# Four re-orderings in a two-layer decoder trunk: memory heads' products inside the last RWKV chunk, two low-part subtractions on POOL, POOL's bonus work gated by VectorE's splits, and five smaller moves

## The reference

```python
for i in range(DEPTH):
    hn = rmsnorm(h, pre_mix_g[i])
    if i % 2 == 0:
        proj = hn @ nsa_w_in[j];   prim = nsa_mixer(...)
    else:
        proj = hn @ rwkv_w_in[j];  prim = rwkv7_time_mix(...)
    mo = memory_attention(proj[..., -MEM_WIDTH:], mem_k, mem_v)
    mix = jnp.concatenate([prim, mo], axis=-1) @ w_out[i]
    h = h + rmsnorm(mix, post_mix_g[i])
    gu = rmsnorm(h, pre_ffn_g[i]) @ w_ffn_in[i]
    ff = (jax.nn.silu(gu[..., :FFN_HIDDEN]) * gu[..., FFN_HIDDEN:]) @ w_ffn_out[i]
    h = h + rmsnorm(ff, post_ffn_g[i])
```

## Time and profile before

| | us |
|---|---|
| median of 3 runs | 733.96 (733.24 to 736.04) |
| the profiled execution's own time | 732.03 |
| its span | 729.9 |
| PE busy | 701.5 (96%) |
| DVE busy | 478.2 (66%) |
| ACT busy | 407.1 (56%) |
| POOL busy | 128.8 (18%) |
| PE clock granted | 0.998 of full |
| one weight piece split: ACT's high part, DVE's low part (means) | 1.88, 2.28 |
| from one 512-column matmul to the next on PE, output products | 0.23 |

### The profile page before, as it was taken

The page is one execution under the profiler, slowest core; times in us unless marked ns, Lnnn a source line. Parts: engine busy times, 40 slices in busy tenths (PEclk is TensorE's granted clock), DMA queues, the critical chain, the costliest instruction groups (busy, mean ns, idle before and its releaser), DMA issues.

```text
span 729.9 us, 14047 instructions
## 1 busy us (share of the span) xinstructions
PE 701.5 (96%) x5949; PEld 606.7 (83%) x5949; DVE 478.2 (66%) x673; ACT 407.1 (56%) x667; POOL 128.8 (18%) x175
## 2 busy tenths in 40 slices
PE   8999989999999999999999999888999999999996
PEld 7879965778888888888889989887789888888885
DVE  4697788747866756633666987985668775666323
ACT  4753868647664554532798945433268555455411
POOL 8111067700000000000180066930000000000000
PEclk9999999999999999999999999999999999999999
DMA  9946810008656555545573531000075665555511
GB/s 303 347 149 200 290 59 2 1 1 276 215 182 206 190 172 190 213 174 172 189 230 116 174 117 60 5 3 4 1 248 188 203 199 173 181 209 187 178 54 57
DMA packets 78288, 111.63 MB, mean 153 GB/s; under 512 B 2140, under 2 KB 64754, under 8 KB 78226
## 3 DMA queue, kind: packets, MB, share of 16 engines
q1 hardware_dynamic: 77170, 107.68, 44.1%
q0 software_dynamic: 976, 3.04, 1.3%
q10 hardware_dynamic: 80, 0.02, 0.0%
HBM read 109.68 MB, written 1.05 MB: 152 GB/s over the span
## 4 chain that ended last, share of the span: by engine, by line
PE 84%; DVE 7%; ACT 4%; issue 2%; POOL 1%; DMA 1%; ACTq 0%; DVEq 0%; POOLq 0%
PE ps L1074 20%; PE ps L746 14%; PE ps L747 13%; PE ps L748 13%; PE ps L1077 10%; DVE w_lo L1925 2%; ACT w_hi L1465 2%; PE ps L1249 2%; PE ps L1267 2%; PE ps L929 2%; PE ps L903 1%; PE ps L878 1%; DMA rows_a<-pre_ffn_g 1%; POOL chunk_x L728 1%; PE ps L1275 1%
## 5 line engine op out<-in xcount | busy, mean ns | idle before, releaser
L1925 DVE TENSOR_TENSOR w_lo<-w_raw,w_hi 128x2048 fp32r<-128x2048 f32 (+3 forms) x102 | 231.5, 2283 | 102.0 <-ACT w_hi L1465 101.9
L1465 ACT ACTIVATE w_hi<-w_raw 128x2048 fp32r<-128x2048 f32 (+3 forms) x102 | 189.4, 1877 | 50.0 <-PE ps L748 45.3
L1074 PE MATMUL ps<-x_hi_lo,w_hi 128*128 128x512 f32 x640 | 201.2, 396 | 0.0
L1077 PEld LDWEIGHTS ps<-x_hi_lo,w_lo 128*128 128x128 f32 x640 | 120.2, 188 | 28.4
L1077 PE MATMUL ps<-x_hi_lo,w_lo 128*128 128x256 f32 x640 | 125.7, 278 | 0.0
L1074 PEld LDWEIGHTS ps<-x_hi_lo,w_hi 128*128 128x128 f32 x640 | 97.4, 189 | 0.0
L746 PE MATMUL ps<-w_hi,x_hi_lo 128*128 128x512 f32 (+3 forms) x240 | 83.0, 346 | 6.1 <-DVE x_hi_lo L2145 4.4
L747 PE MATMUL ps<-w_lo,x_hi_lo 128*128 128x512 f32 (+3 forms) x240 | 81.0, 337 | 0.0
L748 PE MATMUL ps<-w_hi,x_hi_lo 128*128 128x512 f32 (+3 forms) x240 | 81.0, 337 | 0.0
L746 PE MATMUL ps<-w_hi,hidden_hi 128*128 128x512 f32 x176 | 68.6, 390 | 0.0
L747 PE MATMUL ps<-w_lo,hidden_hi 128*128 128x512 f32 x176 | 68.5, 389 | 0.0
(11 more groups left out here) (378 smaller groups left out, 1063.4 us busy)
## 6 DMA issues: line engine op xcount, KB each, us to landing
w_raw<-w_ffn_in SPq DMA_DIRECT2D x44, 1024.0 KB, 5.1
w_raw<-w_ffn_out SPq DMA_DIRECT2D x22, 1024.0 KB, 4.9
w_raw<-rwkv_w_in SPq DMA_DIRECT2D x11, 1024.0 KB, 5.7
w_raw<-w_out SPq DMA_DIRECT2D x8, 1024.0 KB, 4.9
w_raw<-nsa_w_in SPq DMA_DIRECT2D x6, 1024.0 KB, 13.8
w_raw<-nsa_cmp_k_w SPq DMA_DIRECT2D x2, 1024.0 KB, 5.4
w_raw<-nsa_cmp_v_w SPq DMA_DIRECT2D x2, 1024.0 KB, 5.4
w_raw<-nsa_w_in SPq DMA_DIRECT2D x2, 768.0 KB, 4.8
```

Of the source, the lines that this page charges most:

```text
L1074: pe.matmul(psum[:, bank + j, :], kt_of(w_hi, i, k)[:, cols[j]], xx[:, k, :, :].rearrange("p c n -> p (c n)"), start=k == 0, stop=False)
L1077: ins = pe.matmul(psum[:, bank + j, 0:SEQ], kt_of(w_lo, i, k)[:, cols[j]], xh[:, k, :], start=False, stop=k == KD - 1)
L1465: act.activation(w_hi[:, i % SPL, 0:size(i)], raw[:, i % RAW, 0:size(i)], ACT.Copy).then_inc(hi_done, 1)
L1925: dve.tensor_tensor(w_lo[:, i % RAW, 0:size(i)], raw[:, i % RAW, 0:size(i)], w_hi[:, i % SPL, 0:size(i)], ALU.subtract).then_inc(lo_done, 1)
```

## The change

- PE, last chunk: the memory heads' twelve matmuls for tile 0 are taken out of `out_pieces([(0, 0)])` and spread: three before the wait for `k_zs`, three behind `turn_y(1)` (itself moved ahead of the wait for `k_us`), six behind the last y product. `turn_y(2)` moves from before piece (1, 0) to behind it.
- ACT and DVE, last chunk: `high(0)` moves to right behind the copy of z, `high(1)` ahead of `gn_square(3)`; `finish_lo(0)`, `finish(1)` and `finish_lo(1)` move ahead of `gn_mean(3)`.
- Joins 0 and 2: the low part of the second strip's piece is made by POOL (`low_part`), and DVE only waits for its count later.
- All three joins: tile 1's transposes move from behind tile 0's strips to before the last six matmuls of the second of them.
- POOL's bonus work waits until DVE has made the low parts of the two pieces in front of W1.
- ACT does one split, the four A copies, and then the other two splits.

The hunks below stand in the order of the file: POOL's program, PE's, ACT's, DVE's.

```diff
+            def low_part(i):
+                pool.wait_ge(hi_done, i + 1)
+                pool.wait_ge(lo_done, i)
+                pool.tensor_tensor(w_lo[:, i % RAW, 0:size(i)], raw[:, i % RAW, 0:size(i)], w_hi[:, i % SPL, 0:size(i)],
+                                   ALU.subtract).then_inc(lo_done, 1)
...
             scale_probs(0)
+            low_part(first["out", 0] + N_OUT + 1)
             load_gain(1)
...
             pool.wait_ge(g_ev, 3)
+            pool.wait_ge(lo_done, first["rwkv"] + 11 + 3 + AHEAD - 1)
             for f in range(FT):
                 ins = pool.tensor_scalar(rT[:, f, :], rT[:, f, :], colB[:, B_LNB + f:B_LNB + f + 1], None, ALU.add)
...
             ins.then_inc(gb_ok, 1)
+            low_part(first["out", 1] + N_OUT + 1)
             load_gain(3)
...
                         pe.wait_ge(j_lo, tile_base(m, t) + k // 2 + 1)
+                    if t == 0 and part == 1 and k == KD - 2:
+                        norm_tile(m, 1)
...
                 for t in range(TT):
-                    if t:
-                        norm_tile(m, t)
                     for part in range(2):
...
+            def memory_rows(part, nh):
+                kk = 2 * OUT_PAIRS[1][0] + part
+                three(psum[:, acc_bank(2, 0) + nh, :], xh[:, kk, tile(0)], xl[:, kk, tile(0)],
+                      kt_of(w_hi, first["out", 1], part)[:, HALVES[nh]], kt_of(w_lo, first["out", 1], part)[:, HALVES[nh]],
+                      start=part == 0, stop=False)
...
-                if c >= 3:
-                    pe.wait_ge(y_fin_ok, c - 2)
+                if c == NCH - 1:
+                    pe.wait_ge(lo_done, first["out", 1] + 1)
+                    memory_rows(0, 0)
+                    pe.wait_ge(y_fin_ok, 1)
                 pe.wait_ge(k_zs, c + 1)
                 each(U_BANK, inv(c), z_in).then_inc(k_u, 1)
...
+                if c == NCH - 1:
+                    turn_y(1)
+                    memory_rows(1, 0)
                 pe.wait_ge(k_us, c + 1)
...
-                if c == 3:
-                    turn_y(1)
-            out_pieces([(0, 0)])
+            memory_rows(0, 1)
+            memory_rows(1, 1)
+            pe.wait_ge(y_lo, 2)
+            out_pieces([(1, 0)])
             turn_y(NCH - 2)
-            pe.wait_ge(y_lo, 2)
-            out_pieces([(1, 0), (2, 0)])
+            out_pieces([(2, 0)])
             turn_y(NCH - 1)
...
-            split_to(first["rwkv"] + 11 + 3)
+            split_to(first["rwkv"] + 11 + 1)
...
                 act.activation(x2[:, c, 0], six(2 * c), ACT.Copy).then_inc(pa[c], 1)
+            split_to(first["rwkv"] + 11 + 3)
...
                 act.activation(by_pair(zt[:]), crossed(z_at(c)), ACT.Copy).then_inc(k_zs, 1)
+                if c == NCH - 1:
+                    high(0)
...
-            high(0)
+            high(1)
             gn_square(NCH - 1)
-            high(1)
             gn_root(NCH - 1)
...
                     if t == 0:
-                        split_to(last_piece + 2)
                         first_half(m, 1)
                     tile_lo(m, t)
+                if m != 1:
+                    dve.wait_ge(lo_done, last_piece + 2)
+                    split[0] += 1
                 split_to(last_piece + 5)
...
                     finish(0)
+                if c == NCH - 1:
+                    finish_lo(0)
+                    finish(1)
+                    finish_lo(1)
                 gn_mean(c)
                 if c:
                     gn_scale(c - 1)
-            finish_lo(0)
-            finish(1)
-            finish_lo(1)
             gn_variance(NCH - 1)
```

## The result

| | before | after |
|---|---|---|
| median, executions of the comparison | 733.96 (732.06 to 736.04, 5) | 723.35 (722.86 to 725.32, 5) |
| ratio to before, 95% interval | | 0.9852 (0.9835 to 0.9869) |
| the profiled execution: own time, span | 732.03, 729.9 | 725.32, 723.6 |
| its granted clock | 0.998 | 0.994 |

The kernel became 10.6 us faster by the medians.

What follows compares the result with a forecast made beforehand. PE's own work was taken to bound the kernel, so only its idle time could be won. Terms -2.8, -2.4, -0.3, -2.95 and +0.1 gave -8.3: 732.03 to 723.7, plus 1.9 for the median, 725.7 us; range 723.7 to 729.8.

Steps and rivals of the forecast that it cites:

- Part 1: Last chunk: memory products fill PE's four gaps, together 2.93 us, and DVE's new order keeps up; -2.8 (-1.4 to -2.9).
- the late y: Last chunk: the last y product starts at about 511.5 instead of 510.95, 0.5 us late.
- both covers: Last chunk: inputs ready just ahead of PE, by 0.15 us at piece (1, 0) and 0.2 at tile 1.
- part 4: Ahead of W1: with POOL's bonus work later, DVE's splits shorten and PE's wait of 2.97 goes; -2.95 (0 to -3.0).
- Parts 2 and 3: Joins: POOL's low parts and earlier transposes win 1.2 each in joins 0 and 2; transposes win 0.3 in join 1.
- Part 5: Ahead of V1: POOL may issue before DVE's splits, V1's first sum then starting later; +0.1 (-0.3 to +0.5).
- (a): Last chunk gives back half, `y_lo` of 2 and 4 being late: -1.4 in place of -2.8, 727.1; chance 0.15.
- (b): Joins 0 and 2: POOL's low part ends late and delays `h` of tile 1; 729.1 us, chance 0.08.
- (c): Ahead of W1: part 4 does nothing, or bonus work holds W1 or the masks; 728.7 us, chance 0.06.
- (d): Joins 0 and 2: POOL's low part takes 10.6 us, each join loses 4.4; slower, 736.8 us, chance 0.03.
- (e): Whole kernel: low bounds of all terms, some 0.5 us more, with the medians' scatter; 724.5 us, chance 0.05.
- the clock theory: From the experiments: PE's long gaps also bring falls of the granted clock, costing 1.6 us more; no chance given.

Runs made afterwards that it cites:

- experiment 6: Kernel after with four extra POOL subtractions of 256 columns ahead of POOL's low part in joins 0 and 2: 728.5 us, those joins 2.22 longer each.
- experiment 2: Kernel after with POOL's bonus work no longer held back: 727.84 us in one run.
- experiment 1: Both kernels again, unaltered: after 722.87 us, ratio 0.9854; before 733.99 us, ratio to itself 1.0006.
- experiment 4: Kernel after with the last chunk and the start of the output product in the order of before: 728.06 us.
- experiment 8: Kernel before with idle matmuls ahead of W1's consumers alone, 734.08 us, or in the last chunk alone, 733.9; kernel after with POOL's bonus work ungated, 728.13.
- the kernel with both fills: Kernel before with 18 unread identity matmuls in PE's gaps, 12 ahead of W1's consumers and 6 in the last chunk: 732.5 us, ratio 0.9977.
- experiment 7's second kernel: Kernel after with the last chunk in the order of before, timed again: 726.09 us (725.66 to 727.44).
- both single fills: Kernel before with only the 12 idle matmuls ahead of W1's consumers, 734.08 us (ratio 1.0008), or only the last chunk's 6, 733.9 (1.0003).

## Why the prediction was right in kind and too small

- **Part 1, last chunk** (-2.8): all four gaps filled, the late y as described, both covers held. Measured -3.09. The term was mis-sized by 0.29: it took the gaps at their brackets, 2.93, less 0.15 for changes of shape. A bracket counts from the modelled end of the last matmul, and a row of 0.39 whose successor starts 0.23 later shows that this end can lie 0.16 behind the point from which the next could have started. The one gap of part 4 shows it plainly: 2.97 by its bracket, 3.12 won. How much of the 0.29 is this and how much the 0.15 isn't shown. The Trainium skill (Perfetto Trace Analysis, "Tensor Engine Instruction (MATMUL, LD_WEIGHTS)") says that this end is an estimate, and the rows agree.
- **Parts 2 and 3, joins** (-1.2, -0.3, -1.2): measured -1.16, -0.25, -1.15. POOL's instruction was sized by subtracting the wait inside a row (4.5, measured 4.61); the plain proportion of the same row would have said 6.7, an ending 2.1 later than the measured one, and experiment 6 shows what an ending 2.7 later costs.
- **Part 4** (-2.95): measured -3.12, for the same reason as part 1. The cause of the long split was named rightly: experiment 2 undoes it.
- **Part 5** (+0.1): measured -0.21. The order of the two engines was foreseen, its effect not: the price was put on DVE's first sum, but PE's path goes over POOL's fourth product, which ends 0.3 earlier. The forecast took that end for unchanged.
- **Rivals (a) to (d)** didn't occur: no wait in the last chunk, none for POOL's low part, no cover lost. Rival (e), more than forecast, is what came; its 724.5 was still 1.15 too high.
- **The step that failed** is the last of the sum: "it lay 1.9 below the median of the runs, 733.96, from which the prediction goes". These 1.9 us were carried over whole to the kernel after, as if every kernel's median lay that far above its undisturbed execution. Over all executions the kernel before has its median 2.27 above its fastest (733.98 against 731.71, 75 executions; the profiled one, at 732.03, was among its fastest tenth), the kernel after only 0.82 (722.90 against 722.08, 9 executions).
- **The 2.35 us in full**: 0.65 are the terms (-9.0 measured, -8.35 forecast), 0.45 lie outside the span, where the sum had no term at all, 0.09 are two roundings up (8.35 to 8.3, 725.6 to 725.7), and 1.16 are left for the carried distance, the start up to join 0 included.
- **Why the distance shrank** is in part argued. That some executions with these gaps pay for a fall of the clock right behind them is seen in traces (experiments 1, 2, 4 and 8), and the executions at a mean clock of 0.990 or less, 21 of 70 before, are absent from the kernel after and from the kernel with both fills. Against it stand the timings of experiment 7's second kernel and of both single fills: none came out as the clock theory had it. Falls ahead of join 0 are a second source: 7 of the 16 profiles have one at 96 to 107 us, kernels with the change among them, so with nine executions of the kernel after a part of the difference may be chance.

Left open: why one fill alone has no effect, why the same gap is followed by a fall in some executions and not in others, and what shortens the time outside the span. The low end of the range should have held the result: 723.7 was the forecast's own figure for the profiled execution, without room for the terms' small errors to add up.

## What to carry to other kernels

When one profile lies at the edge of the times of its kernel, the distance from the median isn't a constant that a change leaves alone: look at the granted clock in windows of several profiles, and at the time outside the span, before carrying either over. When DVE and POOL both work from SBUF, read an overlong row as work plus a wait for the other engine's instruction, subtract the wait before pricing the row elsewhere, and find which engine's last instruction the path goes over; here the pair ahead of W1, pulled apart, gave 3.1 of its 3.2 us of waiting, and one split less ahead of V1 gave 1.3 of 2.0. A cover of 0.3 us was enough, but beyond it the loss was nearly one for one.

## What the hardware did that I had not expected

- The granted clock of a PE that is 96% busy falls to 0.50 (1.2 of 2.4 GHz) for some 3 to 7 us, in part of the executions of the same program. In two profiles it came about 1 us behind gaps of 1.06 to 1.08 and 0.54 (experiments 1, 4), in two at the end of one of 2.96 (experiments 2, 8), at a price of 1.5 to 1.6 us each. Others lay at 8 to 15 us (3 of the 16 profiles) and at 96 to 107 us (7 of them), in stretches whose code the change doesn't touch; those profiles reach join 0 up to 3 us later than the earliest. The first profile of the kernel after has one there (windows below), and its span is 3.2 us above that of the second:

```profile
100.00:102.00 2.00, 1.64 (x8) 0.83 (x6) 1.97 (x6) 1.56 (x7) 2.00 (x3) 0.50 0.00 0
102.00:104.00 2.00, 1.96 (x8) 1.07 (x7) 1.83 (x9) 1.68 (x7) 2.00 (x3) 0.50 0.00 0
104.00:106.00 2.00, 2.00 (x14) 1.44 (x12) 1.83 (x8) 0.00 (x0) 0.64 (x1) 0.50 0.03 8
```

- POOL's subtraction of 2048 numbers took 4.57 to 4.61 us, twice DVE's 2.28, and yet it costs nothing where POOL is idle and DVE has no instruction with two SBUF inputs to start.
- The time of an execution outside its span is 0.45 us shorter with POOL's `low_part` than without (1.67 to 1.79 against 2.11 to 2.24, no overlap in 138 executions).
